# Output weights split during the last projection blocks, their remainders by VectorE, and a first output tile in two sweeps

## The reference, cut to what matters

```
pa = ya @ w_proj_a                    # (512, 512)  x (512, 1024)
pb = yd @ w_proj_b                    # (512, 1024) x (1024, 1024)
ga, gb = split(sigmoid(gm))           # gm: the last 2048 columns of h @ w_in
y = (ga * pa + gb * pb) @ w_out       # (512, 1024) x (1024, 1024)
y = rms_norm(y, norm_post)
return x + gate * y
```

## Time and profile before

| | us |
|---|---|
| median of 3 runs | 929.48 |
| lowest, highest | 927.55, 931.8 |
| the profiled execution | 928.42 |
| its span in the trace | 926.6 |

### The profile page before, as it was taken

How to read it: one execution, slowest core, us unless ns; L and a number is a source line. 1 busy time by engine, 2 the same in 40 slices (tenths; PEclk the granted TensorE clock), 3 DMA queues, 4 the chain that set the end, 5 groups by cost and what they waited for, 6 DMA issues and landing times.

```text
span 926.6 us, 12694 instructions
## 1 busy us (share of the span) xinstructions
PE 834.0 (90%) x4622; PEld 696.0 (75%) x4622; DVE 463.1 (50%) x785; ACT 358.1 (39%) x777; POOL 494.5 (53%) x657
## 2 busy tenths in 40 slices
PE   1578799999999999998988879998899999999797
PEld 1568589888878788788767757875788777888697
DVE  2866377463534344322467767757756644212122
ACT  4233344444434343423434334543545632222311
POOL 2674445353464555335767674744546537638900
PEclk9989799999989999999988999999999999999899
DMA  9763372233233323222533222222122113323421
GB/s 256 212 185 92 108 267 81 69 91 104 68 104 103 103 69 108 83 96 80 170 96 92 87 74 69 80 80 69 58 69 65 50 46 114 114 69 123 150 73 65
DMA packets 89716, 94.77 MB, mean 102 GB/s; under 512 B 5133, under 2 KB 80950, under 8 KB 89526
## 3 DMA queue, kind: packets, MB, share of 16 engines
q1 hardware_dynamic: 89360, 93.54, 33.1%
q0 software_dynamic: 240, 0.39, 0.4%
q10 hardware_dynamic: 54, 0.02, 0.0%
HBM read 78.11 MB, written 5.34 MB: 90 GB/s over the span
## 4 chain that ended last, share of the span: by engine, by line
PE 42%; POOL 17%; DVE 13%; DMA 9%; ACT 7%; issue 7%; SPq 5%; ACTq 0%; DVEq 0%; POOLq 0%
PE proj L1465 29%; POOL w_lo L671 9%; PE proj L1548 4%; DMA rope_s<-rope_x 4%; POOL rope_x L696 3%; DVE rope_o L1076 3%; SPq L551 3%; PE score L1344 2%; DMA ada<-in_w_ada 2%; PE sums L1390 2%; PE turned L1361 2%; ACT w_hi L785 1%; DVE ada_sum L1006 1%; POOL h_lo L671 1%; PE score L1319 1%
## 5 line engine op out<-in xcount | busy, mean ns | idle before, releaser
L671 POOL TENSOR_TENSOR w_lo<-raw,w_hi 128x256 fp32r<-128x256 f32 x408 | 321.7, 820 | 245.0 <-ACT w_hi L785 244.9
L1465 PE MATMUL proj<-h_hi,w_hi 128*128 128x512 f32 x608 | 255.2, 420 | 10.2 <-POOL h_lo L681 7.9
L1465 PE MATMUL proj<-h_hi,w_lo 128*128 128x512 f32 x608 | 243.5, 401 | 0.0
L1465 PE MATMUL proj<-h_lo,w_hi 128*128 128x512 f32 x608 | 243.2, 400 | 0.0
L1465 PEld LDWEIGHTS proj<-h_hi,w_hi 128*128 128x128 f32 x608 | 117.8, 194 | 46.0 <-POOL h_lo L681 9.3
L1465 PEld LDWEIGHTS proj<-h_hi,w_lo 128*128 128x128 f32 x608 | 117.7, 194 | 26.7
L1465 PEld LDWEIGHTS proj<-h_lo,w_hi 128*128 128x128 f32 x608 | 118.1, 194 | 21.4
L785 ACT ACTIVATE w_hi<-raw 128x1024 fp32r<-128x1024 f32 x102 | 106.0, 1055 | 12.8 <-PE proj L1465 7.7
L696 POOL TENSOR_TENSOR rope_x<-rope_x,cos_t 128x512 f32<-128x512 f32 x36 | 53.9, 1496 | 84.8 <-DMA rope_s<-rope_x 84.4
L1139 DVE TENSOR_TENSOR at_lo<-turned,at_hi 128x512 fp32r<-128x512 f32 x64 | 44.1, 689 | 67.5 <-ACT at_hi L887 65.2
L1390 PE MATMUL sums<-v,at_hi 128*128 128x128 f32 (+1 forms) x256 | 63.1, 316 | 14.4 <-DVE at_lo L1139 14.2
(11 more groups left out here) (236 smaller groups left out, 1545.6 us busy)
## 6 DMA issues: line engine op xcount, KB each, us to landing
raw<-in_w_in SPq DMA_DIRECT2D x88, 512.0 KB, 3.6
rope_s<-rope_x SPq DMA_DIRECT2D x144, 64.0 KB, 2.3
ada<-in_w_ada SPq DMA_DIRECT2D x16, 512.0 KB, 6.2
zd<-in_w_ada SPq DMA_DIRECT2D x8, 512.0 KB, 4.9
raw<-in_w_proj_b SPq DMA_DIRECT2D x8, 512.0 KB, 3.4
raw<-in_w_out SPq DMA_DIRECT2D x8, 512.0 KB, 3.4
rows_in<-window_rows SPq DMA_DIRECT2D x4, 792.0 KB, 4.5
window_rows<-rows_out SPq DMA_DIRECT2D x4, 528.0 KB, 4.9
```

Of the source, the lines that this page charges most:

```text
L671: ins = nc.gpsimd.tensor_tensor(lo[:, k, :], raw[:, n % RAW, k, :], hi.bitcast(F32)[:, k, :], ALU.subtract)
L1465: ins = mm(dst, left, right, start=k == 0 and n == 0, stop=k == nk - 1 and n == 2)
```

## The change

Four edits:

1. Order of rounding. w_out's eight halves are now (54,0) at tick 189, (54,1) and (55,0) at 194, (55,1) at 195, (52,0) and (52,1) at 196, (53,0) at 197, (53,1) at 198. None is left behind the last tick.
2. Their remainders are made by VectorE (`out_lo`), one TENSOR_TENSOR of 128x1024 for each half, and no longer by GpSimd. GpSimd keeps the remainders of the input blocks and g_lo. SP waits for the engine that frees the raw buffer.
3. Places. Block 52 goes to the memory of ya (free after the last w_proj_a tile), block 53 to block 50's half of w_hi/w_lo.
4. TensorE's first output tile takes contraction rows 0 to 5 for all four column blocks, then 6 and 7 for all four. Its first wait on `ab_mixed` asks only for the two banks that it writes. The accumulation of a bank starts once, not once for each column block.

```
-    for b in range(3, NB + 1):
+    for b in range(3, NB):
...
-    for n, q in zip((6, 7, 10, 11), ((NB + 2, 0), (NB + 2, 1), (NB + 3, 0), (NB + 3, 1))):
+    out_ticks = (1, 6, 6, 7, 8, 8, 9, 10)
+    for n, q in zip(out_ticks, ((b, h) for b in (NB + 2, NB + 3, NB, NB + 1) for h in range(2))):
         prep.setdefault(start_tick[NB - 4] + n, []).append(q)
-    prep.setdefault(LAST_TICK + 1, []).extend([(NB + 1, 0), (NB + 1, 1)])
...
-            if b < NB + 2:
+            if b < NB:
                 return [w[:, b % 2, 4 * h:4 * h + 4, :] for w in (w_hi, w_lo)]
-            flat = [w[:].rearrange("p k s -> p (k s)") for w in (h_hi, h_lo)]
+            if b == NB + 1:
+                return [w[:, NB % 2, 4 * h:4 * h + 4, :] for w in (w_hi, w_lo)]
+            flat = [w[:].rearrange("p k s -> p (k s)") for w in (ya if b == NB else (h_hi, h_lo))]
...
                 if n >= RAW:
-                    sp.wait_ge(w_lo_done, 4 * (n - RAW + 1))
+                    old = halves[n - RAW]
+                    if old[0] < NB:
+                        sp.wait_ge(w_lo_done, 4 * (pool_no[old] + 1))
+                    else:
+                        sp.wait_ge(out_lo_done, out_no[old] + 1)
...
                 for half in prep_at(t) if t >= 12 else []:
-                    cut_lo(half)
+                    if half[0] < NB:
+                        cut_lo(half)
...
+                if b == NB:
+                    act.wait_ge(proj_done, max(t.u for t in tiles if t.kind == "a") + 1)
+                if b == NB + 1:
+                    act.wait_ge(proj_done, max(t.u for t in tiles if t.b == NB - 2) + 1)
...
+            def out_lo(half):
+                dve.wait_ge(w_hi_done, half_no[half] + 1)
+                hi, lo = w_place(half)
+                tt_(lo, raw[:, half_no[half] % RAW, :, :], hi.bitcast(F32), ALU.subtract).then_inc(out_lo_done, 1)
...
                 for tile in tiles_done(t):
                     leave_bank(tile)
+                for half in prep_at(t):
+                    if half[0] >= NB:
+                        out_lo(half)
...
-            for tt in range(NT):
-                if tt == 0:
-                    pe.wait_ge(ab_mixed, max(MIXED.values()))
-                for n_b, b in enumerate((NB + 2, NB + 3, NB, NB + 1)):
...
+            def out_products(tt, n_b, ks):
...
+                for k in ks:
+                    if tt == 0 and k % 4 == 0:
+                        pe.wait_ge(out_lo_done, out_no[b, k // 4] + 1)
+                    if tt == 0 and n_b == 0:
+                        pe.wait_ge(g_lo_done, k + 1)
...
+            pe.wait_ge(ab_mixed, max(MIXED[t.u] for t in tiles[-4:-2]))
+            for n_b in range(4):
+                out_products(0, n_b, range(KT - 2))
+            for n_b in range(4):
+                out_products(0, n_b, range(KT - 2, KT))
+            pe.wait_ge(ab_mixed, max(MIXED.values()))
+            for tt in range(1, NT):
```

More of the change, by code:

```diff
@@ L174, in build @@
         prep.setdefault(-1, []).append(q)
-    for b in range(3, NB + 1):
-        nk = blocks[b].nk if b < NB else KT
-        for h in range(nk // 4):
+    for b in range(3, NB):
+        for h in range(blocks[b].nk // 4):
             prep.setdefault(start_tick[b - 1] + h, []).append((b, h))
-    for n, q in zip((6, 7, 10, 11), ((NB + 2, 0), (NB + 2, 1), (NB + 3, 0), (NB + 3, 1))):
+    out_ticks = (1, 6, 6, 7, 8, 8, 9, 10)
+    for n, q in zip(out_ticks, ((b, h) for b in (NB + 2, NB + 3, NB, NB + 1) for h in range(2))):
         prep.setdefault(start_tick[NB - 4] + n, []).append(q)
-    prep.setdefault(LAST_TICK + 1, []).extend([(NB + 1, 0), (NB + 1, 1)])
     prep_at = lambda t: prep.get(t, [])
@@ L185, in build @@
     half_no = {q: n for n, q in enumerate(halves)}
+    pool_no = {q: n for n, q in enumerate(q for q in halves if q[0] < NB)}
+    out_no = {q: n for n, q in enumerate(q for q in halves if q[0] >= NB)}
     for b in range(NB):
@@ L378, in build @@
         w_lo_done = sem("w_lo_done")
+        out_lo_done = sem("out_lo_done")
         rope_cos_done = sem("rope_cos_done")
@@ L477, in w_place @@
                 return [block2_hi[:, 4 * h:4 * h + 4, :], block2_lo[h][:]]
-            if b < NB + 2:
+            if b < NB:
                 return [w[:, b % 2, 4 * h:4 * h + 4, :] for w in (w_hi, w_lo)]
-            flat = [w[:].rearrange("p k s -> p (k s)") for w in (h_hi, h_lo)]
-            at = (b - NB - 2) * KT * BW + h * 4 * BW
+            if b == NB + 1:
+                return [w[:, NB % 2, 4 * h:4 * h + 4, :] for w in (w_hi, w_lo)]
+            flat = [w[:].rearrange("p k s -> p (k s)") for w in (ya if b == NB else (h_hi, h_lo))]
+            at = max(b - NB - 2, 0) * KT * BW + h * 4 * BW
             return [w[:, at:at + 4 * BW].rearrange("p (k n) -> p k n", k=4) for w in flat]
@@ L753, in _ @@
                                             g_hi[:, n, :].bitcast(F32), ALU.subtract).then_inc(g_lo_done, 1)
-            for half in prep_at(LAST_TICK + 1):
-                cut_lo(half)
             for tt in range(NT):
@@ L779, in cut_hi @@
                 act.wait_ge(raw_loaded[n % RAW], 16 * (n // RAW + 1))
-                if 3 <= b < NB + 2:
+                if 3 <= b < NB:
                     before = max(t.u for t in tiles if t.b == (b - 2 if b != 4 else 0))
                     act.wait_ge(proj_done, before + 1)
+                if b == NB:
+                    act.wait_ge(proj_done, max(t.u for t in tiles if t.kind == "a") + 1)
+                if b == NB + 1:
+                    act.wait_ge(proj_done, max(t.u for t in tiles if t.b == NB - 2) + 1)
                 if b >= NB + 2:
@@ L959, in _ @@
                         nc.scalar.activation(g_hi[:, n, :], gates[:, tile.which % 2, tile.j, :], ACT.Copy).then_inc(g_hi_done, 1)
-            for half in prep_at(LAST_TICK + 1):
-                cut_hi(half)
             for tt in range(NT):
@@ L1445, in products @@
                     if tile.j == 0:
-                        pe.wait_ge(w_lo_done, 4 * half_no[tile.b, k // 4] + k % 4 + 1)
+                        pe.wait_ge(w_lo_done, 4 * pool_no[tile.b, k // 4] + k % 4 + 1)
                     if tile.kind == "b" and tile.b == B_FIRST and tile.j == 0:
@@ L1531, in _ @@
                     vt_turn(tile)
-            for tt in range(NT):
-                if tt == 0:
-                    pe.wait_ge(ab_mixed, max(MIXED.values()))
-                for n_b, b in enumerate((NB + 2, NB + 3, NB, NB + 1)):
+            OUT = (NB + 2, NB + 3, NB, NB + 1)
+            def out_products(tt, n_b, ks):
+                b = OUT[n_b]
+                col = (b - NB) * BW
+                dst = proj[:, 2 * (tt % 2):2 * (tt % 2) + 2, :].rearrange("p a s -> p (a s)")[:, col:col + BW]
+                for k in ks:
[3 more added lines that the diff above has]
+                        pe.wait_ge(g_lo_done, k + 1)
+                    hi, lo = w_place((b, k // 4))
+                    for n, (a, c_) in enumerate(PASSES):
+                        ins = mm(dst, (g_hi, g_lo)[a][:, k, tt * P:(tt + 1) * P], (hi, lo)[c_][:, k % 4, :],
+                                 start=k == 0 and n == 0 and n_b % 2 == 0, stop=k == KT - 1 and n == 2,
+                                 skip_group_check=True)
+                if n_b % 2 and ks[-1] == KT - 1:
+                    ins.then_inc(y_done, 1)
@@ L1537, in _ @@
+            assert len(tiles) % 4 == 0
+            pe.wait_ge(ab_mixed, max(MIXED[t.u] for t in tiles[-4:-2]))
[5 more added lines that the diff above has]
+            for tt in range(1, NT):
+                for n_b in range(4):
                     if tt >= 2 and n_b % 2 == 0:
                         pe.wait_ge(y_read, 2 * (tt - 2) + n_b // 2 + 1)
-                    col = (b - NB) * BW
@@ L1540, in _ @@
[L1540 to L1549, removed]
@@ L1550, in _ @@
-                    if n_b % 2:
-                        ins.then_inc(y_done, 1)
+                    out_products(tt, n_b, range(KT))
 _INS = ['x', 'c', 'positions', 'w_ada', 'b_ada', 'norm_pre', 'w_in', 'lambda_q1', 'lambda_k1',
```

## The result

| | before | after |
|---|---|---|
| median of 6 runs, us | 929.14 | 918.96 |
| lowest, highest | 925.41, 932.12 | 916.29, 920.79 |
| profiled execution, us | 928.42 | 918.94 |
| its span | 926.6 | 917.1 |
| POOL busy | 494.5 | 470.2 |

The ratio after to before is 0.9885, with a 95% interval of 0.9857 to 0.9912. 919.0 was predicted, from 917.2 to 921.5, and a gain of 9.7 us on the profiled execution, which gained 9.5. Four executions of the groups further down (one of the kernel before, one of e5_late_order, two of e10_late_one) took 1038 to 1826 us and are left out of every median and ratio given here; only the 1.7 us in the expectation of e5_again counts one in.

A forecast was written before the change was run, and what follows sets the result against it. GpSimd's remainders of w_out and the gated rows were taken to bound the end of the b blocks. Late start 0.95, waits 2.85 and 3.5, slow clock 2.1, restarts 0.3 give 9.7: 928.42 - 9.7 = 918.7, predicted 919.0, range 917.2 to 921.5.

The forecast's parts named there:

- the hole: End of the b blocks into tile 0: TensorE waits for GpSimd's remainders; closing this gains 9.7 us.
- Part 1: Tile 0 on TensorE: two sweeps want row 6 only at 874.05; the narrower ab_mixed wait gains 0.95 us.
- Part 2: Rows 6 and 7: g_lo of row 7 done by 869.9 at the latest, 4.5 us ahead of need.
- bad case: Subtractions at 1.75 us: (53,1) and the start of tile 115's product at 868.2, row 7 done at 872.3.
- Part 3: w_out's remainders on VectorE: eight subtractions, 1.27 us each where GpSimd is quiet, 1.75 where busy; they fit.
- Part 4: Ring of raw-buffer loads: one place less costs nothing; (53,1) done by 865.7, with 5 us cover even at 868.2.
- Rival D: A gap moves forward: (50,1) misses 846.1, costing about 1 us, 919.7 to 920.5; chance included in the forecast's 0.86.
- A: Late remainders, with 6.2 us loads and 1.75 us subtractions, stop TensorE 3.5 us: 922.2 to 924.4; chance 0.07.
- B: Same ring, loads from about 7.4 us: tile 0 ends at 887.3, 0.5 after before, so slower; chance 0.02.
- Rival C: Behind tile 0, stores or VectorE freeing banks are already due, so closing the hole gains nothing: 928 stays; chance 0.05.

The follow-up runs named there:

- e5_late_order: The changed kernel with the old order of rounding, block 53 behind the last tick: 921.96 us, ratio to before 0.9920.
- e10_late_one: The changed kernel with the old order of rounding and one sweep, narrow wait kept: 922.50 us, ratio to before 0.9927.
- e5_again: The changed kernel with the old order of rounding, run again beside the changed kernel: 919.69 us, ratio to before 0.9899.
- e4: The changed kernel with the wide wait on ab_mixed ahead of tile 0, as before the change: 926.52 us, ratio to before 0.9949.
- e6: The changed kernel with each of VectorE's eight subtractions made twice in series: 924.62 us, ratio to before 0.9959.
- e7: The changed kernel with each of VectorE's eight subtractions made three times: 938.61 us, ratio to before 1.0087.
- e2: The kernel before with only the two sweeps and the narrow wait, GpSimd making all remainders in the old order: 925.53 us, ratio to before 0.9962.
- e3: The changed kernel with w_out's remainders made by GpSimd again, order, places and sweeps as changed: 926.76 us, ratio to before 0.9958.
- e1: The changed kernel with tile 0 in one sweep, rows 0 to 7 for each column block in turn: 925.79 us, ratio to before 0.9954.
- e8: The kernel before with VectorE's remainders and the new places only (old order, one sweep, wide wait): 922.45 us, ratio to before 0.9922.

## Why the prediction was right

- **What bounds, and the worth of the hole.** Right in mechanism and size: the stage fell by 9.70 us, as computed. That three gaps and a slow clock would go together because nothing refills them is what the trace after shows.
- **Part 1, two sweeps.** The waits for rows 6 and 7 are hidden as said. The 0.95 for the narrow wait is the price in the kernel before. In the changed one it is 4.25 (e4), because the same change puts a subtraction ahead of tile 115's product and the clock falls behind the longer gap. The prediction named that queue, but priced the edit only against before.
- **Part 2, rows 6 and 7.** 869.9 was called the latest for row 7, with tile 115's product starting at 865.73; it started at 867.82 and the row was done at 871.26. The bad case of part 4 (868.2 and 872.3) holds it. The detail that was wrong is "the product of tile 115 still starts at 865.73"; the cover hid it.
- **Part 3, the subtractions.** 1.27 to 1.75 us were taken; they took 1.21 to 1.47. The term was slightly too high, and the bad case's 1.75 did not occur.
- **Part 4, the ring.** (53,1) at 867.9 was forecast between 865.7 and 868.2, but the bad case came there by subtractions of 1.75 us and loads of 3.4. The runs show subtractions of 1.23 and last loads of 4.3 and 5.3, at a DMA share of 0.83. That 867.9 lies in the band is luck: one term was too high, the other too low. The cost of the ring's lost place for the b blocks is zero, as said: no gap in 842 to 866. Rival D did not happen.
- **Rivals A and B.** Neither happened. e6 and e7 show that the ring can do it, by slow subtractions; slow loads, the cause that A and B name, were not tried. Twice the subtraction costs 3.7 us, near A's 3.5 at the full clock (A allowed 5.7 at the half clock, which did not come), and three times makes the kernel slower than before, with the clock's fall, as in B. B has a slip: tile 0's slots ended at 886.6 before (the square at 886.83 comes 0.2 later), so its 887.3 is 0.7 later, not 0.5.
- **Rival C.** Excluded: later tiles are still 11.40 and 11.38 us apart, 11.36 before, and the time fell.
- **The total.** 9.5 us on the profiled execution, 10.2 between the medians; the 919.0 lay 0.04 beside the median, which is closer than the scatter of 2 us between groups of runs allows anyone to claim.

What the prediction did not see is how unequal the edits are: it argued for the whole, and the whole closes the hole, but VectorE's remainders (with the new places, not separated by a run) do five sixths of it, and the early order does none and costs 3.0 us where the sweeps don't cover for it.

## What to carry to other kernels

When an engine in the chain is full and a neighbour is idle, move the work over first and measure; reordering around the full engine (e2, e3) recovered less than half. Edits that look independent aren't when they share a queue: the value of a narrower wait or another product order (0 to 4.6 us here) depends on what stands ahead of the awaited instruction, so price an edit in the kernel that it will live in, also by taking it out again. Where buffers are handed round, give the delay of one turn times the turns in series, and keep the cover in view: here 3.3 us, used up by 1.25 us more for each subtraction.

## What the runs showed of the hardware

- A single gap of TensorE cost more than itself. After gaps of 2.5 and 2.8 us (e4, e1) it went on at full pace, and then 16 matmuls ran at the clock's lower level (granted 0.50, 1.2 GHz), 1.5 us more. After a gap of 3.1 us (e3) the clock was at its lower level from the first matmul on, for 28 matmuls. After a gap of 1.3 us (e10), two of 0.8 and 0.3 (e8), and three of 0.2, 0.7 and 2.0 (e6) the clock stayed at its upper level and the cost was the gap.
- A subtraction of VectorE stands still while GpSimd subtracts. In e6 this one started while GpSimd's g_lo ran:

```profile
872.41 1.54 POOL L755 TENSOR_TENSOR g_lo<-gates,g_hi 128x512 fp32r<-128x512 f32 x1 [7.95 <-ACT g_hi L970]
...
872.83 2.21 DVE L1224 TENSOR_TENSOR w_lo<-raw,w_hi 128x1024 fp32r<-128x1024 f32 x1
```

It took 2.21 us, not 1.22: the rest of g_lo was 1.12, and 0.99 is what it lost. The one at 863.34 in the same run, beside the g_lo of 862.91 to 864.46, also took 2.21. The page "SBUF — State Buffer" of the Trainium skill, section "SBUF: two separate sides", calls the ports that the two engines share an exclusive lock: whichever starts first has them for the whole instruction. By that rule the subtraction would lose the 1.12 us that g_lo had left, and the trace agrees to 0.13 us. In the changed kernel it cost little (1.47 us at most for a subtraction), as g_lo was all that GpSimd had left behind 851.
